# Reordering the opening of a hybrid MLA / RG-LRU encoder block: the latent columns' product first, token tile by token tile

## The reference

```python
h = rmsnorm(x, norm1_g[l])
proj = h @ w_in[l]
q_a = proj[..., :256]
kv_a = proj[..., 256:384]
k_rope_raw = proj[..., 384:416]
lru_x = proj[..., 416:928]
lru_y = proj[..., 928:1440]
gate_logits = proj[..., 1440:]

attn = mla_mixer(q_a, kv_a, k_rope_raw, ...) @ w_o_attn[l]      # 8 heads
rec = rglru_bidir(lru_x, conv_w[l], ...)                        # 4 blocks, 2 directions
rec = (jax.nn.gelu(lru_y) * rec) @ w_o_lru[l]
merged = sigmoid(gate_logits[..., :D]) * attn + sigmoid(gate_logits[..., D:]) * rec
x = x + merged @ w_out[l]
h2 = rmsnorm(x, norm2_g[l])
x = x + (silu(h2 @ w_ffn_gate[l]) * (h2 @ w_ffn_up[l])) @ w_ffn_down[l]
return rmsnorm(x, final_g)
```

## Time and profile before

| what | value |
|---|---|
| median of 3 runs | 677.28 us (677.25 to 677.99) |
| the profiled execution | 679.51 us |
| its span in the trace | 677.7 us |
| PE busy | 663.3 us, 98% of the span |
| DVE, ACT, POOL busy | 78%, 59%, 12% of the span |
| granted clock of PE, mean | 0.997 |

### The profile page before, as it was taken

How to read it: one execution, slowest core, us unless ns; L and a number is a source line. 1 busy time by engine, 2 the same in 40 slices (tenths; PEclk the granted TensorE clock), 3 DMA queues, 4 the chain that set the end, 5 groups by cost and what they waited for, 6 DMA issues and landing times.

```text
span 677.7 us, 10940 instructions
## 1 busy us (share of the span) xinstructions
PE 663.3 (98%) x4006; PEld 593.1 (88%) x4006; DVE 527.4 (78%) x823; ACT 399.5 (59%) x670; POOL 78.6 (12%) x80
## 2 busy tenths in 40 slices
PE   6999999999999999999999999999999999999996
PEld 6998888888888878888899999999999998778884
DVE  4595647888788886873579997888777769799896
ACT  5436678797777874232565644455554456556573
POOL 1000401011222110000000000000000004304342
PEclk9999999999999999999999999999999999999998
DMA  7324102222222226334062444422444317999903
GB/s 249 122 77 126 54 24 73 69 72 68 62 72 69 103 70 236 120 125 124 3 178 72 125 125 125 112 75 66 120 124 124 124 46 178 238 267 171 171 1 124
DMA packets 83314, 75.94 MB, mean 112 GB/s; under 512 B 6415, under 2 KB 67022, under 8 KB 83278
## 3 DMA queue, kind: packets, MB, share of 16 engines
q1 hardware_dynamic: 77246, 63.93, 31.3%
q0 software_dynamic: 6016, 11.54, 9.5%
q10 hardware_dynamic: 16, 0.00, 0.0%
HBM read 73.37 MB, written 2.10 MB: 111 GB/s over the span
## 4 chain that ended last, share of the span: by engine, by line
PE 80%; DVE 7%; issue 6%; DMA 4%; ACT 2%; POOL 1%; SPq 0%; POOLq 0%; DVEq 0%; ACTq 0%
PE ps L475 15%; PE ps L476 15%; PE ps L477 15%; PE ps L1890 8%; PE ps L1893 8%; PE ps L1892 8%; PE ps L1963 2%; PE ps L1965 2%; PE ps L1967 2%; DMA scr<-in_w_ffn_down_dram 2%; PE ps L1799 2%; DVE w_lo L1389 1%; DMA raw<-in_w_in_dram 1%; DVE f_lo L1384 1%; PE ps L1749 1%
## 5 line engine op out<-in xcount | busy, mean ns | idle before, releaser
L475 PE MATMUL ps<-hT_hi,w_lo 128*128 128x512 f32 (+1 forms) x288 | 100.3, 348 | 3.5 <-DVE hT_lo L1114 3.0
L476 PE MATMUL ps<-hT_lo,w_hi 128*128 128x512 f32 (+1 forms) x288 | 98.6, 342 | 0.0
L477 PE MATMUL ps<-hT_hi,w_hi 128*128 128x512 f32 (+1 forms) x288 | 98.5, 342 | 0.0
L319 DVE TENSOR_TENSOR w_lo<-raw,w_hi 128x1024 fp32r<-128x1024 f32 (+3 forms) x55 | 64.2, 1172 | 36.2 <-ACT w_hi L309 35.1
L1890 PE MATMUL ps<-f_hi,w_lo 128*128 128x256 f32 x320 | 90.7, 283 | 0.0
L1893 PE MATMUL ps<-f_hi,w_hi 128*128 128x256 f32 x320 | 90.6, 283 | 0.0
L1892 PE MATMUL ps<-f_lo,w_hi 128*128 128x256 f32 x320 | 90.6, 283 | 0.0
L309 ACT ACTIVATE w_hi<-raw 128x1024 fp32r<-128x1024 f32 (+3 forms) x55 | 53.8, 987 | 41.1 <-PE ps L477 36.5
L957 ACT ACTIVATE w_hi<-scr 128x1024 fp32r<-128x1024 f32 x50 | 51.9, 1056 | 37.8 <-PE ps L1893 33.4
L1890 PE MATMUL ps<-hT_hi,w_lo 128*128 128x256 f32 x240 | 67.9, 283 | 0.0
L1892 PE MATMUL ps<-hT_lo,w_hi 128*128 128x256 f32 x240 | 67.9, 283 | 0.0
(11 more groups left out here) (219 smaller groups left out, 1559.9 us busy)
## 6 DMA issues: line engine op xcount, KB each, us to landing
raw<-in_w_in_dram SPq DMA_DIRECT2D x12, 1024.0 KB
raw<-in_w_ffn_gate_dram SPq DMA_DIRECT2D x12, 512.0 KB, 4.5
raw<-in_w_ffn_up_dram SPq DMA_DIRECT2D x12, 512.0 KB, 5.0
raw<-in_w_ffn_down_dram POOLq DMA_DIRECT2D x12, 512.0 KB, 9.8
scr<-in_w_ffn_down_dram SPq DMA_DIRECT2D x11, 512.0 KB, 8.0
scr<-in_w_ffn_gate_dram SPq DMA_DIRECT2D x10, 512.0 KB, 5.2
scr<-in_w_ffn_up_dram SPq DMA_DIRECT2D x10, 512.0 KB, 5.9
raw<-in_w_out_dram SPq DMA_DIRECT2D x4, 1024.0 KB
```

The costliest lines, as they stand in the source:

```text
L319: last = nc.vector.tensor_tensor(split_view(w_lo, kind, t0 % 4), raw_view(kind, t0 // 2 % 2, t0 % 2), split_view(w_hi, kind, t0 % 4).bitca ...
L475: nc.tensor.matmul(dst, l_lo, r_hi, start=start, stop=False)
L476: nc.tensor.matmul(dst, l_hi, r_lo, start=False, stop=False)
L477: return nc.tensor.matmul(dst, l_hi, r_hi, start=False, stop=stop)
```

## The change

The latent columns' product moves to the front. Its weights (T_A) are now loaded in four quarters between the x tiles. It goes token tile by token tile. For the first token tile PE makes two passes over the eight row blocks, first all products with the high weights, then those with the low weights, and the transposes of the second token tile stand in the middle of the second pass. Of the other token tiles' transposes, two stand behind every second product. The lru_x tiles follow, at their full width of 512 tokens, then two lru_y tiles with the latent transposes between them, the gates of direction 0, the other lru_y tiles, the values and the gates of direction 1. POOL casts three of the four high latent weights, and makes the power and the scaling of x tiles 1 to 3; the power of the latent norm is POOL's too, where before ACT took a root and DVE refined it. The unread transposes are 20 in place of 30. Only the rows of tile 0 are still scaled by DVE.

```diff
-T_X, T_A, T_G0, T_Y, T_V, T_G1 = 0, 4, 8, 10, 14, 15
+T_A, T_X, T_G0, T_V, T_G1 = 0, 4, 10, 14, 15
+T_Y = (8, 9, 12, 13)
...
         def gate_bank(d, part, n):
-            return (4 if d != part else 0) + n
+            return ((4, 5, 6, 7), (2, 3, 0, 1), (0, 1, 4, 5), (6, 7, 2, 3))[2 * d + part][n]
+
+        Y_BANK = (0, 1, 4, 5)
+        V_BANK = (6, 7, 2, 3)
...
             load_x(0)
+            load_a(0)
+            load_a(1)
             load_x(1)
-            load_lru_x(0)
+            load_a(2)
+            load_a(3)
             load_x(2)
             load_x(3)
-            load_lru_x(1)
...
-            for half in range(2):
-                pool.wait_ge(mse_ready, half + 2)
-                power(rstd[:, 0, 2 * half:2 * half + 2], mse[:, 0, 2 * half:2 * half + 2], 2, pow_ready)
+            pool.wait_ge(mse_ready, 1)
+            power(rstd[:, 0, 0:1], mse[:, 0, 0:1], 1, pow_ready)
...
+                nc.gpsimd.tensor_copy(split_view(w_hi, "a", t), raw_view("a", t // 2, t % 2)).then_inc(a_half, 1)
+
+            def scaled_rows(t):
+
+                pool.wait_ge(ssq_ready, t + 1)
+                link(nc.gpsimd.tensor_scalar(mse[:, 0, t:t + 1], ssq[:, 0, t:t + 1], EPS, None, ALU.add))
+                link(nc.gpsimd.tensor_tensor(rstd[:, 0, t:t + 1], mse[:, 0, t:t + 1], nhalf[:, 0:1], ALU.pow))
+                nc.gpsimd.tensor_scalar(xt[:, t, :], xt[:, t, :], rstd[:, 0, t:t + 1], None, ALU.mult).then_inc(xs_ready, 1)
+
+            for t in range(1, 4):
+                a_hi(t)
+            for t in range(1, NT):
+                scaled_rows(t)
...
+            def h_hi(t):
+                for d in range(KD):
+                    act.wait_ge(xT_done, 4 * t + d // 2 + 1)
+                    nc.scalar.activation(hT_hi[:, d, P * t:P * t + P], x_turned(d), ACT.Copy,
+                                         scale=prm[:, ROW_G1 + d:ROW_G1 + d + 1]).then_inc(h_half, 1)
...
-            square_sum(xt[:, 0, :], 0, 0, sq_junk[:, 0, :], scale=float(D) ** -0.5)
-            act.wait_ge(x_in[1], 16)
-            square_sum(xt[:, 1, 0:512], 0, 1, sq_junk[:, 1, 0:512], scale=float(D) ** -0.5)
-            split_hi(act, 0)
+            square_sum(xt[:, 0, 0:512], 0, 0, sq_junk[:, 0, 0:512], scale=float(D) ** -0.5)
+            split_hi(act, T_A)
             act.wait_ge(prm_ready, 1)
-            norm_hi(ROW_G1, 4, 0, 0, h_half)
-            split_hi(act, 1)
-            for t in (2, 3):
+            h_hi(0)
+            for t in range(1, NT):
                 act.wait_ge(x_in[t], 16)
-                square_sum(xt[:, t, :], 0, t, sq_junk[:, t % 2, :])
-            split_hi(act, 2)
-            split_hi(act, 3)
-            norm_hi(ROW_G1, 4, 1, 0, h_half)
-
+                square_sum(xt[:, t, :], 0, t, sq_junk[:, t % 2, :], scale=float(D) ** -0.5)
+                if t > 1:
+                    h_hi(t - 1)
+            h_hi(NT - 1)
...
+            dve.wait_ge(pow_ready, 1)
+            nc.vector.tensor_scalar(xt[:, 0, :], xt[:, 0, :], rstd[:, 0, 0:1], None, ALU.mult).then_inc(xn_ready, 1)
+            h_lo(0)
+            for n in range(4):
+                split_lo(dve, T_A + n)
+
+            nc.vector.sem_inc(w_half, 3)
+            h_lo(1)
+            keep_a(0)
...
-            for n in range(30):
+            for n in range(20):
                 nc.tensor.transpose(ps[:, 6, 0:P], ident[:, :], ident[:, :])
             pe.wait_ge(prm_ready, 1)
-            transpose_half(xt, 0, 0, 4)
-            norm_and_tiles(xt, 0, 4, T_X, 0, h_ready)
-            pe.wait_ge(prm_ready, 2)
...
+            for k in range(KD):
+                x_hi, x_lo, wh, wl = a_views(0, k)
+                if k % 2 == 0:
+                    pe.wait_ge(w_ready, T_A + k // 2 + 1)
+                last = nc.tensor.matmul(ps[:, 0, 0:CA], x_hi, wl, start=False, stop=k == KD - 1)
+                if k == 3:
+                    transpose_rows(1)
+            last.then_inc(a_done, 1)
+            for t in range(1, NT):
+                for k in range(KD):
+                    pe.wait_ge(h_ready, KD * t + k + 1)
+                    last = product(ps[:, t, 0:CA], *a_views(t, k), k == 0, k == KD - 1)
...
+                    if t < NT - 1 and k % 2:
+                        transpose_rows(t + 1, (k // 2,))
+            pe.wait_ge(prm_in, 16 * 8)
+            nc.tensor.transpose(ps[:, 7, 0:N_ROWS], rows[0:N_ROWS, :], ident[0:N_ROWS, 0:N_ROWS]).then_inc(prm_t, 1)
+            for n in range(NB):
+                if n == 3:
+                    pe.wait_ge(prm_ready, 2)
+                used(cols_tile(T_X + n, 0, 4 + n))
...
-            pe.wait_ge(xp_ready, NB)
+            pe.wait_ge(pa_ready, 1)
+            used(cols_tile(T_Y[0], 0, Y_BANK[0]))
+            pe.wait_ge(pa_norm, NT)
...
+            pe.wait_ge(pa_ready, 2)
+            used(cols_tile(T_Y[1], 0, Y_BANK[1]))
+            pe.wait_ge(aT_ready, 4)
             lru_gates(0, T_G0)
...
+            for m in (2, 3):
+                pe.wait_ge(sig_ready, m - 1)
+                used(cols_tile(T_Y[m], 0, Y_BANK[m]))
...
-            pe.wait_ge(sig_ready, 14)
+            pe.wait_ge(sig_ready, 2 * NB + 2)
             q_and_k(0, 0)
```

More of the change, by code:

```diff
@@ L526, in load_lru_gates, with load_lru_y @@
                          src[:, d, :, :], inc=inc if part else 16)
-            load_lru_gates(4, 0, 0, 32)
-            for p in (5, 6):
-                load(p, 0, k_major(p, KD), w_in_v[:, :, C_LY + 256 * (p - 5):C_LY + 256 * (p - 5) + 256])
+            def load_lru_y(p, half):
+                load(p, 0, k_major(p, KD), w_in_v[:, :, C_LY + 256 * half:C_LY + 256 * half + 256])
+            load_lru_y(4, 0)
+            load_lru_gates(5, 0, 0, 32)
+            load_lru_y(6, 1)
             load_lru_gates(7, 1, 1024, 16)
@@ new lines, in _ @@
+            nc.vector.tensor_scalar(xt[:, 0, :], xt[:, 0, :], rstd[:, 0, 0:1], None, ALU.mult).then_inc(xn_ready, 1)
[5 more added lines that the diff above has]
+            keep_a(0)
+            h_lo(2)
+            keep_a(1)
+            h_lo(3)
+            keep_a(2)
+            for n in range(3):
+                split_lo(dve, T_X + n)
+            keep_a(3)
+            split_lo(dve, T_X + 3)
@@ L1216, in _ @@
[L1216 to L1224 removed]
+            split_lo(dve, T_V)
@@ L1630, in transpose_half, with transpose_rows @@
                             ins.then_inc(xT_done, 1)
+            def transpose_rows(t, pairs=range(KD // 2)):
+                pe.wait_ge(xs_ready if t else xn_ready, t if t else 1)
+                for b in pairs:
+                    for d in (2 * b, 2 * b + 1):
+                        ins = nc.tensor.transpose(x_turned(d), xt[:, t, P * d:P * d + P], ident[:, :])
+                    ins.then_inc(xT_done, 1)
             def half_tile(t0, bank, half, h_sem=None):
@@ L1642, in half_tile @@
                 return last
-            def norm_and_tiles(src, count, base, t0, bank, h_sem):
-                for j in range(4):
-                    half_tile(t0 + j, bank + j, 0, h_sem if not j else None)
-                    if j == 1:
-                        transpose_half(src, count, 1, base)
-                for j in range(4):
-                    used(half_tile(t0 + j, bank + j, 1, h_sem if not j else None))
-                    if j == 0:
-                        pe.wait_ge(prm_in, 16 * 8)
-                        nc.tensor.transpose(ps[:, 7, 0:N_ROWS], rows[0:N_ROWS, :],
-                                            ident[0:N_ROWS, 0:N_ROWS]).then_inc(prm_t, 1)
@@ new lines, in a_views @@
+            def a_views(t, k):
+                n, tok = k // 2, slice(P * t, P * t + P)
+                return (hT_hi[:, k, tok], hT_lo[:, k, tok],
+                        split_view(w_hi, "a", n)[:, k % 2, :], split_view(w_lo, "a", n)[:, k % 2, :])
+            for k in range(KD):
+                x_hi, x_lo, wh, wl = a_views(0, k)
+                if not k:
+                    pe.wait_ge(w_half, 1)
+                elif k % 2 == 0:
+                    pe.wait_ge(a_half, k // 2)
+                if k % 2 == 0:
+                    pe.wait_ge(h_half, k + 2)
+                nc.tensor.matmul(ps[:, 0, 0:CA], x_hi, wh, start=k == 0, stop=False)
+                pe.wait_ge(h_ready, k + 1)
+                nc.tensor.matmul(ps[:, 0, 0:CA], x_lo, wh, start=False, stop=False)
```

302 lines of the change are left out of this document (160 added, 142 removed).

## The result

The changed kernel takes 679.37 us (median of 7 runs, 678.74 to 680.74), the kernel before 677.33 (7 runs): the ratio is 1.0027, with a 95% interval of 1.0018 to 1.0036. It is slower, by 1.2 to 2.4 us, where 3.7 us less had been forecast. Its profiled execution took 678.74 us, around a span of 676.9.

What follows compares the result with a forecast made beforehand. PE, busy 98% of the span, was taken to bound the kernel; its dense stretch starting at 16.1 gave 3.5 us, reordering 0.3 saved and 0.1 lost: 677.28 - 3.7 = 673.6 us, range 671.7 to 676.4.

Steps and rivals of the forecast that it cites:

- the scaling by GpSimd: Opening, x tile 1: 1.1 us taken between bounds of 1.03 and 2.6, 1.6 beside DVE's splits, ending at 14.1.
- addition, power and the two steps between them 0.9: Opening, GpSimd behind its third cast: these small steps take 0.9 us, from 11.6 to 12.5.
- rival B: Opening: no contention between GpSimd and DVE, and quarters land as by bytes; tile 1 at 14.3, 671.8 us; chance 0.08.
- the x tiles 2 and 3 are scaled 2.0 to 2.5 us apart: Opening: PE takes 4.5 + 0.9 us per tile, so these rows are ready in time.
- Rival A: Opening: GpSimd's scaling takes 2.6 us, stretched to 3.7; tile 1 at 18.2, gain 1.6, 675.7 us; chance 0.17.
- rival C: Opening: TensorE's clock does not stay up, some 5.6 us at half speed cost 2.8; 676.4 us; chance 0.08.
- rival D: Reordered gates before the head loop: the gain is given back, ACT 5.6 us later than worked out; about 677.3; chance 0.05.
- Rival E: Opening: every tile waits for GpSimd's per-tile chain, measurably slower from 5.4 us each; 680.5 at 6 us; chance 0.06.
- the difference carries over: Baseline: the 3.7 us gained before the head loop in the trace comes off the median 677.28, giving 673.6.
- does lie on the path: Opening: shortening the warm-up from 30 to 20 transposes, 0.20 us each, lets tile 0's transposes start at 6.5.

Runs made afterwards that it cites:

- forms: Changed kernel with POOL multiplying x tile 2 by a constant and overwriting tile 3 by a plain copy, tile 1 scaled as before; no kernel time given.
- fill34: Changed kernel plus 34 unread transposes on PE ahead of tile 1's transposes; 678.89 us, ratio to before 1.0026.
- fill_all: Changed kernel plus unread transposes in every hole of token tile 0's product (3, 10, 10 and 28); 679.11 us, ratio to before 1.0026.
- dve_scale: Changed kernel with the scaling of x tiles 1 to 3 on DVE in place of POOL; 675.72 us, ratio to before 0.9971.
- tile1_only: Changed kernel with only x tile 1's scaling on DVE, tiles 2 and 3 staying on POOL; 677.17 us, ratio to before 0.9993.
- best2_fill: best2 plus 14 unread transposes ahead of the wait for the third high weight; 674.09 us, ratio to before 0.9948.
- best4: best2 with x tile 1 loaded behind the third latent weight quarter, plus 8 and 6 unread transposes; 673.89 us, ratio to before 0.9945.
- best2: Changed kernel with x tile 1 scaled and the fourth weight cast by ACT, tiles 2 and 3 scaled by DVE, among other edits; 674.52 us, ratio 0.9954.

## Why the prediction was wrong, step by step

**Right:** tile 0's scaling done by 6.4 (6.55), its transposes from 6.5 (6.76), DVE's low halves until 10.1 (10.3), a cast of 832 columns in 0.87 (0.88), the sixth transfer in at 10.6 (the cast behind it starts at 10.69), DVE's last split by 14.5 to 15 (14.86), and the 77.4 us from tile 1's first product to the head loop (77.3).

**Wrong, the decisive step:** "the scaling by GpSimd". The prediction took 1.1 us "as it reads one tensor, like the copy", between bounds of 1.03 and 2.6, and 1.6 with the stretch. It took 2.86 alone and 3.14 here, above the upper bound too. The run forms shows that reading one tensor does not make a multiplication cheap. Per column it is 2.8 ns, beside 2.5 for the two-input multiplication of the earlier trace rows and 1.0 for a copy. The Trainium skill, GPSIMD Engine Reference, section Engine selection, says that one-input work runs at roughly line-rate on GpSimd, and two-input work about twice slower than on VectorE. The copy agrees with that; the multiplication, nearly four times DVE's 0.75 us, does not.

**Wrong, the second step:** "addition, power and the two steps between them 0.9". From the cast's end at 12.12 to the scaling's start it took 2.34. The prediction stretched the scaling and the casts by 1.44 and left the short steps as they were. In fact the scaling grew by 10%, the addition fourfold, the power twofold, and the third cast from 0.88 to 1.43. So the contention that rival B denied was there, but as 0.3 to 0.7 us for each instruction and not as a factor. Taken one by one, the subtractions show how:

```profile
11.30 1.69 DVE L327 TENSOR_TENSOR w_lo<-raw,w_hi 128x832 fp32r<-128x832 f32 x1
12.92 1.01 DVE L327 TENSOR_TENSOR w_lo<-raw,w_hi 128x832 fp32r<-128x832 f32 x1
```

The addition that began beside the first of these ended 0.1 us behind its end (13.09 and 12.99), the power beside the second 0.4 us behind (14.36 and 13.93). The same 0.1 and 0.4 stand in the second trace of the changed kernel and in those of fill34, fill_all, dve_scale and tile1_only. It holds the other way too: the first of the two, begun beside the cast, took 1.69 us and ended 0.9 behind the cast (12.99 and 12.12). So in these traces the one that starts later seems to be held until the other is through. No run takes the subtractions away by themselves.

The sum for tile 1's rows was 11.6 + 0.3 + 0.9 + 1.6 = 14.4, and became 12.12 + 2.34 + 3.14 = 17.60, 3.2 later: 0.2 by the casts, 1.4 by the small steps and 1.5 by the scaling. From there to the first product the prediction had 1.7 us; it took 2.7, with the clock at half (1.63 at full clock, from the transposes' start in fill_all). Together 4.2, and 4.1 of it reached the head loop.

**Wrong, the third step:** "the x tiles 2 and 3 are scaled 2.0 to 2.5 us apart", and so "ready in time". They came 3.9 apart (the scalings end at 17.60 and 21.50). In the changed kernel that is hidden behind tile 1's lateness and the fall of the clock; the runs fill_all and tile1_only show it, with 0.66 and 1.34 us of wait.

**Rivals taken one by one.** Rival A (slow scaling, 675.7) was the right mechanism, with 2.1 of the 5.8 us by which the forecast missed; rival C (the clock, 676.4) happened as well, though in this kernel it cost 0.6, since POOL's second tile was next. It came by rival A's wait: in the trace of dve_scale, with the same 20 unread transposes and the same first pass, the clock stayed at 1.00. Each was priced as if the rest of the forecast held. Rival B fell with the stretched casts and steps, rival D with the 77.3 us to the head loop. Rival E, the slower one, was bound to three chains of 5.4 us each, with a wait for every tile. Only the first took that long (12.21 to 17.60), the next 3.8, and PE waited for tile 1 alone. That the kernel is slower all the same has to do with the place from which the gain was counted, which is the next point.

**Wrong, the baseline:** "the difference carries over". The traced execution of before took 679.51 us against a median of 677.28. In the very stage that the change replaces it waited 2.85 us, where the other two traces waited 1.73 and 1.78, and its head loop started at 97.19, against 96.39 and 96.27. Forecasting a gain from 97.19 counted some 0.9 us that these executions don't have to lose; these two still took 0.8 and 0.9 us more than the median, so it may be more. With 96.6 as the mean of the three traces before, and 98.2 as that of the two after, the traces differ by 1.6 us, which is inside the measured 1.2 to 2.4. The miss of 5.8 us adds up so: 4.1 from the head loop's place, 2.2 by which the traced execution of before stood above its median, and 0.6 by which that of the changed kernel stood below its own, less 1.2 because the first trace of before was also longer behind the head loop's start (580.5 against 579.3).

**Small:** the warm-up "does lie on the path" was wrong, and cost nothing: the first pass waits for loads anyway.

That the layout itself was not the fault is shown by best2_fill and best4: the same order of products, with the scaling off POOL and also with one cast and one addition less there, reached tile 1 at 16.05 and 15.83 (forecast 16.1), the head loop at 92.98 and 92.91 (93.5), and a time 0.5% below before, which is what the forecast had given this kernel.

## What to carry to other kernels

An operation that the trace doesn't show is better priced by its arithmetic than by the number of its inputs; where the only near row is a dearer kin (here the multiply at 2.5 ns a column), take that one, or the whole chain hangs on a hope. Where an off-path engine is given a chain of small steps beside a busy neighbour, count each step, not only the long one. And before a difference is taken from one trace, see how far its execution stands from the median, and whether the excess lies in the stage that the change replaces.

## Not expected of the hardware

GpSimd multiplies 1,024 columns by a constant in 2.79 us, by a column in 2.85, and copies them in 1.04. A one-column addition there takes 0.22 us alone, 0.88 beside DVE's two-input subtractions, and 0.78 beside DVE's one-input scaling of 1,024 columns (dve_scale); a power takes 0.57 alone and 1.18 beside subtractions, a cast of 832 columns 0.88 and 1.43. The granted clock fell to half behind holes of 3.7 us (the first trace of the changed kernel) and of 1.9 us (best2), both times while PE was busy again; behind the 2.85 us of the earlier trace rows it did not fall. In the second trace of the changed kernel it fell within the hole: it reads 0.50 from 18.5 to 19 us, and PE was idle until 19.15.
